# A hybrid three-mixer diffusion layer with MoE on one core: recurrence gates directly behind their projections, forget blocks next, output gate products within the HGRN2 levels, and the output projection in rows

## The reference

```python
sh1, sc1, gt1, sh2, sc2, gt2 = split(silu(c) @ ada_w + ada_b, 6)       # one set for context, one for latent
h = rms(x, norm1_w) * (1 + sc1) + sh1
qkv, g, a, b, q_hg, i_hg, g_hg, f_hg, x_rg, y_rg = split(h @ w_in)
o_a = gated_delta_net(qkv, g, a, b)      # 4 heads x 128, both directions
f = lb + (1 - lb) * sigmoid(f_hg)        # HGRN2: 4 heads x 64, both directions
o_b = rms(hgrn2(q_hg, i_hg, log(f))) * silu(g_hg)
u = dwconv(x_rg); r, i = sigmoid(u @ rg_gate_w + b)                    # RG-LRU, width 256
a_t = exp(-8 * r * softplus(-lam)); h_t = a_t * h_(t-1) + sqrt(1 - a_t**2) * (i * u)
o_c = (h_forward + h_backward) * gelu(y_rg)
x = x + gt1 * (concat(o_a, o_b, o_c) @ w_out)
h = rms(x, norm2_w) * (1 + sc2) + sh2
x = x + gt2 * moe(h)                     # 16 experts, top 2 within one group of 4
y = rms(x, final_norm_w)                 # and the final context states of the three mixers
```

## Time and profile before

| what | value |
|---|---|
| median of 3 runs | 1136.64 us (1133.79 to 1137.53) |
| the profiled execution's own time | 1141.2 us |
| its span | 1139.5 us |
| TensorE matmul busy | 944.6 us (83%) |
| VectorE busy | 429.4 us (38%) |
| ScalarE busy | 279.1 us (24%) |
| GpSimd busy | 125.5 us (11%) |
| share of the chain that ended last | TensorE 67%, VectorE 16%, ScalarE 5%, DMA 5%, issue 5% |

### The profile page before, as it was taken

The page is one execution under the profiler, slowest core; times in us unless marked ns, Lnnn a source line. Parts: engine busy times, 40 slices in busy tenths (PEclk is TensorE's granted clock), DMA queues, the critical chain, the costliest instruction groups (busy, mean ns, idle before and its releaser), DMA issues.

```text
span 1139.5 us, 24022 instructions
## 1 busy us (share of the span) xinstructions
PE 944.6 (83%) x10893; PEld 674.9 (59%) x10893; DVE 429.4 (38%) x718; ACT 279.1 (24%) x451; POOL 125.5 (11%) x138
## 2 busy tenths in 40 slices
PE   3799994458999889879999859966799999999930
PEld 3557753356665544678899845536667855765510
DVE  2340076996345233366577441137001000100008
ACT  3320534223112117222222230043201001100114
POOL 1300000000000000163555000000100000000021
PEclk9899997688999899989999969988899999999975
DMA  8990224266020200000000011255479999999835
GB/s 307 395 324 11 74 74 148 76 223 223 5 78 8 85 1 2 1 3 3 21 3 2 3 70 79 74 203 203 164 263 344 403 389 387 397 391 405 333 123 203
DMA packets 54413, 185.22 MB, mean 163 GB/s; under 512 B 8123, under 2 KB 11266, under 8 KB 50210
## 3 DMA queue, kind: packets, MB, share of 16 engines
q1 hardware_dynamic: 39408, 151.13, 34.9%
q0 software_dynamic: 6224, 22.55, 5.9%
q10 hardware_dynamic: 8674, 9.94, 2.5%
HBM read 160.93 MB, written 22.68 MB: 161 GB/s over the span
## 4 chain that ended last, share of the span: by engine, by line
PE 67%; DVE 16%; ACT 5%; DMA 5%; issue 5%; POOL 1%; ACTq 1%; DVEq 0%; POOLq 0%; SPq 0%
PE ps L657 19%; PE ps L1104 14%; PE ps L1127 7%; PE ps L925 7%; PE ps L723 6%; PE ps L647 4%; PE ps L913 3%; DMA arena<-in_moe_w_gate 1%; DMA ring<-in_ada_w 1%; PE ps L882 1%; ACT hT L1227 1%; PE ps L1001 1%; DVE arena L1885 1%; PE ps L796 1%; PE ps L1004 1%
## 5 line engine op out<-in xcount | busy, mean ns | idle before, releaser
L657 PE MATMUL ps<-hT,ring 128*128 128x128 f32 (+1 forms) x832 | 231.9, 439 | 3.2 <-ACT hT L1227 1.9
L657 PEld LDWEIGHTS ps<-hT,ring 128*128 128x128 f32 x832 | 126.4, 193 | 101.1 <-issue 96.8
L2310 DVE TENSOR_TENSOR hT<-ps,hT 128x384 f32<-128x384 f32 (+3 forms) x18 | 9.1, 506 | 248.1 <-ACT hT L1541 237.5
L1104 PE MATMUL ps<-ring,arena 128*32 128x128 f32 (+3 forms) x1104 | 87.6, 378 | 2.9 <-issue 1.8
L1104 PE MATMUL ps<-arena 128*32 128x256 f32 (+3 forms) x1360 | 85.5, 394 | 4.8 <-DVE arena L2302 2.5
L1104 PEld LDWEIGHTS ps<-arena 128*32 128x32 f32 (+1 forms) x1360 | 66.5, 114 | 24.4 <-issue 9.2
L1104 PEld LDWEIGHTS ps<-ring,arena 128*32 128x32 f32 (+1 forms) x1104 | 61.3, 118 | 29.0 <-issue 22.2
L723 PE MATMUL ps<-ring,hT 128*128 128x256 f32 (+1 forms) x240 | 69.2, 450 | 0.0
L647 PE MATMUL ps<-ident,arena 128*128 128x128 f32 (+3 forms) x278 | 41.7, 305 | 23.6 <-DVE arena L2086 10.8
L1694 POOL DMA_INDIRECT arena<-h_rows,slot_tok x18 | 16.6, 925 | 404.9 <-PE ps L647 234.6
L723 PEld LDWEIGHTS ps<-ring,hT 128*128 128x128 f32 x240 | 45.6, 190 | 23.7 <-issue 19.6
(11 more groups left out here) (416 smaller groups left out, 1340.0 us busy)
## 6 DMA issues: line engine op xcount, KB each, us to landing
ring<-in_ada_w SPq DMA_DIRECT2D x12, 2048.0 KB, 9.0
arena<-in_moe_w_gate SPq DMA_DIRECT2D x9, 2048.0 KB, 10.7
arena<-in_moe_w_up SPq DMA_DIRECT2D x9, 2048.0 KB, 15.4
arena<-in_moe_w_down SPq DMA_DIRECT2D x9, 2048.0 KB, 20.8
ring<-in_w_in SPq DMA_DIRECT2D x7, 2048.0 KB, 12.6
ring<-in_moe_w_gate SPq DMA_DIRECT2D x7, 2048.0 KB, 12.2
ring<-in_moe_w_up SPq DMA_DIRECT2D x7, 2048.0 KB, 15.4
ring<-in_moe_w_down SPq DMA_DIRECT2D x7, 2048.0 KB, 20.9
```

Of the source, the lines that this page charges most:

```text
L657: last = mm(out, w[:, k, cols], rhs(k)[:, a:b], start=(k == 0), stop=(k == KD - 1))
L1104: last = mm(ps[rows_of(n, g), GU, 512 * i + at:512 * i + at + width], m_xgT[:, b % 2, k, rows_of(n, j)], w[:, k, col:col + width], start=( ...
```

## The change

Four things are moved, and one stage is written anew.

1. `rgg` comes directly behind `rgy`; then `hq`, `hf`, one `ada`, `hi`. The slab plan has `hf` in one slab of 512 columns, and `hgate`'s weights get a load of their own into x's old place.
2. `hgate` is cut into five jobs of one tile each, behind the `ada` of levels 0 to 4. `ada` l+5 (before: l+6) follows level l. ScalarE copies `hgate` unchanged within its loop over the levels and applies Silu once, later. The forget gates' clamps, logs and additions go block by block.
3. The output projection is done in rows: ten jobs `("out", half, tile)` with tokens stationary and 512 output columns moving. The residual, the second norm and its scale and shift are done in rows, with the gate, scale and shift vectors loaded by DMA: a new job `modrow` turns them to rows, ScalarE stores them in DRAM, and SP loads them back spread over 128 partitions (`rows_in`), with x itself. `h2T` transposes each finished tile for the router product `logits`. `rms` 1, `router`, `h2row`, `rowvec` and `xrow` are gone.
4. The zero rows for the MoE's unused slots are stored from GpSimd's queue behind the load of `state_gdn` instead of at about 41 us, and the 16 small loads of the RG-LRU gate weights are issued by GpSimd, ahead of its `iota`s, instead of by ScalarE. SP issues the stores of h2, and expert 1 is loaded before the rest of expert 0.

```diff
@@ job_plan
     j += [("rgx", b) for b in range(2)] + [("rgy", b) for b in range(2)]
-    j += [("hq", b) for b in range(2)] + [("hi", n) for n in range(2)] + [("hgate", n) for n in range(2)]
     j += [("rgg", n) for n in range(8)]
-    j += [("hf", n) for n in range(4)]
-    j += [("ada", 4), ("ada", 5), ("adaT", 4)]
+    j += [("hq", b) for b in range(2)] + [("hf", n) for n in range(4)]
+    j += [("ada", 4)] + [("hi", n) for n in range(2)] + [("adaT", 4)]
     for l in range(8):
-        j += [("lev", l, n) for n in range(3)] + [("adaT", 4 + l)] * (l > 0) + [("ada", 6 + l)] * (l < 6)
-    j += [("qkv", 0)] + [("kdt", t) for t in range(NT)]
+        j += [("lev", l, n) for n in range(3)] + [("adaT", 4 + l)] * (l > 0) + [("ada", 5 + l)] * (l < 7) + [("hgate", l)] * (l < NT)
+    j += [("qkv", 0)] + [("kdt", t) for t in range(NT)] + [("modrow", 0)]
...
+def out_order():
+    a, b, c, d, e = ROW_ORDER
+    return [("out", 1, t) for t in ROW_ORDER] + [
+        ("out", 0, a), ("out", 0, b), ("h2T", a), ("out", 0, c), ("logits", a), ("h2T", b), ("out", 0, d), ("out", 0, e),
+        ("h2T", c), ("logits", b), ("h2T", d), ("logits", c), ("h2T", e), ("logits", d), ("logits", e)]
@@ SP
+            sp.wait_ge(*full_after(LAST[("out", 1)]))
+            first_expert(0, 1)
+            for n, t in enumerate(ROW_ORDER):
+                if t == ROW_ORDER[-1]:
+                    sp.wait_ge(*full_after(LAST[("out", 0)]))
+                    first_expert(0, 2)
+                sp.wait_ge(s_h2, n + 1)
+                sp.dma_start(h2_dram[P * t:P * t + P, :], m_h2[:, t, :]).then_inc(s_h2_stored, 16)
@@ ScalarE
+            for dp in range(4):
+                act.wait_ge(s_b_m, dp + 1)
+                ch(A(b_f[:, dp, :], b_f[:, dp, :], ACT.Ln))
+                A(b_Z[0][:, dp, :], b_Z[0][:, dp, :], ACT.Ln, scale=1.0 / LNSPLIT).then_inc(s_b_ln, 1)
             modulation(4)
-            modulation(5)
+            for n in range(2):
+                name = ("hi", n)
...
             for l in range(7):
                 act.wait_ge(s_b_d, l + 1)
                 A(b_f[:, :, :], b_f[:, :, :], ACT.Exp).then_inc(s_b_e, 1)
-                if l:
-                    modulation(5 + l)
+                modulation(5 + l)
+                if l < NT:
+                    name = ("hgate", l)
+                    act.wait_ge(*full_after(name))
+                    A(b_g[:, l, :], bank(name)[:, 0:256], ACT.Copy).then_inc(pair_free[pair(name)], 1)
...
+            def squared(t):
+                act.wait_ge(s_x1, ROW_ORDER.index(t) + 1)
+                r = small[:, 24 + t:25 + t]
+                ch(A(m_h2[:, t, :], x_rows[:, t, :], ACT.Square, accum_out=r))
+                ch.sync()
+                A(r, r, ACT.Sqrt, scale=1.0 / D, bias=small[:, 0:1]).then_inc(s_x1r, 1)
@@ VectorE
+            def x1_half(half, t):
...
+                TT(out=m_h2[:, t, at], in0=bank(name)[:, 0:512], in1=gate_row[min(t, 1)][:, at], op=MULT).then_inc(pair_free[pair(name)], 1)
+                dve.wait_ge(*free_after(name))
+                return TT(out=x_rows[:, t, at], in0=x_rows[:, t, at], in1=m_h2[:, t, at], op=ADD)
+            def h2_row(t):
...
+                link(V.reciprocal(r, r))
+                link(STT(out=m_h2[:, t, :], in0=x_rows[:, t, :], scalar=r, in1=scale_row[min(t, 1)], op0=MULT, op1=MULT))
+                TT(out=m_h2[:, t, :], in0=m_h2[:, t, :], in1=shift_row[min(t, 1)], op=ADD).then_inc(s_h2, 1)
+            dve.wait_ge(s_rows_in, 16 * 8)
...
+            dve.wait_ge(s_h2_stored, 16 * NT)
             link(V.tensor_reduce(m_col[:, 0:NT], m_p[:, :, :], AX.X, MAX))
```

More of the change, by code:

```diff
@@ L708, in _ @@
                 project(("rgy", b), w, slice(256 + P * b, 256 + P * b + P))
+            pe.wait_ge(s_conv_c, 2)
+            pe.wait_ge(s_wg_in, 16 * 16)
+            for n in range(8):
+                name = ("rgg", n)
+                pe.wait_ge(*free_before(name))
+                for a, b, out, g in segs(name):
+                    last = mm(out, c_wg[:, n, :], c_u[:, n % 2, a + 2 * g:b + 2 * g], start=True, stop=True)
+                last.then_inc(pair_full[pair(name)], 1)
             w = slab(("hq", 0))
@@ L713, in _ @@
                 project(("hq", b), w, slice(P * b, P * b + P))
+            w = slab(("hf", 0))
+            pe.wait_ge(*slab_after(("hf", 0)))
+            for n in range(4):
+                project(("hf", n), w, slice(P * n, P * n + P))
             def token_rows(kind, w, col, width, per, tiles=NT):
@@ L815, in _ @@
                 last.then_inc(pair_full[pair(name)], 1)
+            name = ("modrow", 0)
+            pe.wait_ge(s_scl2, 1)
+            pe.wait_ge(*free_before(name))
+            for g in range(2):
+                tr(bank(name)[0:48, P * g:P * g + P], modT[:, :, g])
+                last = tr(bank(name)[0:KD, 256 + P * g:384 + P * g], scl2[:, :, g])
+            last.then_inc(pair_full[pair(name)], 1)
             b_kdr = b_k.rearrange("p a t -> p (a t)").rearrange("p (t c n) -> p t c n", t=NT, c=4)
@@ L1036, in h2_rows, with h2_transposed @@
                 for k in range(KD):
-                    last = tr(bank(name)[:, P * k:P * k + P], hT[:, k, P * t:P * t + P])
+                    last = mm(bank(name)[:, 0:512], mix(k, t), slab(("out", half))[:, k, :], start=(k == 0), stop=(k == KD - 1))
                 last.then_inc(pair_full[pair(name)], 1)
-            for t in range(3):
-                h2_rows(t)
+            def h2_transposed(name):
+                pe.wait_ge(s_h2, ROW_ORDER.index(name[1]) + 1)
+                pe.wait_ge(*free_before(name))
+                for k in range(KD):
+                    last = tr(bank(name)[:, P * k:P * k + P], m_h2[:, name[1], P * k:P * k + P])
+                last.then_inc(pair_full[pair(name)], 1)
@@ new lines, in logits @@
+            def logits(name):
+                n = ROW_ORDER.index(name[1])
+                pe.wait_ge(s_narrow_in, 32)
+                pe.wait_ge(*free_after(("h2T", name[1])))
+                pe.wait_ge(*free_before(name))
+                for k in range(KD):
+                    last = mm(bank(name)[:, 0:NE], h2T[n % 2][:, k, :], cs[:, k, 0:NE], start=(k == 0), stop=(k == KD - 1))
+                last.then_inc(pair_full[pair(name)], 1)
+            for name in out_order():
+                {"out": out_rows, "h2T": h2_transposed, "logits": logits}[name[0]](name)
@@ L1318, in _ @@
             A(small[:, 8:12], small[:, 8:12], ACT.Ln, bias=small[:, 1:2]).then_inc(s_c_ln, 1)
-            for n in range(2):
-                name = ("hgate", n)
-                act.wait_ge(*full_after(name))
-                A(b_g[:, 4 * n:min(NT, 4 * n + 4), :], bank(name)[:, 0:256 * (4 if n == 0 else 1)]
-                       .rearrange("p (t c) -> p t c", c=256), ACT.Silu).then_inc(pair_free[pair(name)], 1)
-            act.wait_ge(s_z_stored, 16 * (1 + len(GAPS)))
             for n in range(8):
@@ L1343, in _ @@
                 allow_slow_non_contiguous=True).then_inc(s_state_stored, 16)
+            for b in range(2):
+                name = ("hq", b)
+                act.wait_ge(*full_after(name))
+                for a, e, out, g in segs(name):
+                    ins = A(b_q[:, b, a:e], out, ACT.Copy)
+                    ch(ins) if g == 0 else ins.then_inc(pair_free[pair(name)], 1)
             act.wait_ge(s_c_done, 1)
@@ new lines, in h2_copied @@
+            def h2_copied(t):
+                n = ROW_ORDER.index(t)
+                if n >= 2:
+                    act.wait_ge(*full_after(("logits", ROW_ORDER[n - 2])))
+                name = ("h2T", t)
+                act.wait_ge(*full_after(name))
+                A(h2T[n % 2], bank(name).rearrange("p (k t) -> p k t", k=KD), ACT.Copy).then_inc(pair_free[pair(name)], 1)
+            for n, t in enumerate(ROW_ORDER):
+                squared(t)
+                if n in (1, 2):
+                    h2_copied(ROW_ORDER[n - 1])
```

342 lines of the change are left out of this document (148 added, 194 removed).

## The result

The changed kernel takes 1143.76 us in the median of 6 executions (1140.93 to 1145.85), the kernel before 1136.39 in 6 executions beside it (1132.53 to 1139.00). The ratio is 1.0062, 95% interval 1.0032 to 1.0092: slower by 0.6%. The forecast was 1140.0, slower the likeliest sign; its mechanism was found in the trace as it was described.

What follows compares the result with a forecast made beforehand. TensorE bounds the kernel first, then a hole, VectorE in the levels, TensorE again from the output projection. +6.5 us behind the levels less 3.1 for projection and routing gives +3.4: median 1140.0 us, range 1134 to 1147 (61%).

Steps and rivals of the forecast that it cites:

- The recurrence and the levels: Up to the levels' first exponential: gain 39.2 us from the earlier recurrence; in the levels: loss 44.1 us, 102.1 against 58.0.
- the turn: One level as a single chain: E, PSUM copy, `ada`, `hgate`, its copy, exponential, Z; 17.3 us for each of four levels.
- No coupling in the levels: Rival, levels: exponential l+1 runs beside PSUM out, levels stay at 9.2 us, total 1098; chance 6%.
- The start: Kernel start: 16 loads ahead of the `iota`s and their 0.25 MB in 256-byte pieces cost +1.3 us (0 to 3).
- 0.3 us for `modrow` and the last exponential: Between the levels and the next stage: 0.3 us added, within that stage's later start of 6.5 us.
- the ring: Levels: ScalarE copies `ada` and `hgate` ahead of the next exponential, so parallel work becomes one chain, 17.3 us a level.
- 12.1 us: Last tile after the output projection, up to the maximum over the logits: 12.1 us, where it was 19.3.
- The output projection's: Output projection in rows: 68.7 us of matmuls, cold start 1.9, -0.5, two `h2T` of 0.95, one `logits` 2.2; ends 3.6 later.
- `hgate` at the lower clock: Rival, levels: `hgate` behind idle time runs slower, 3.1 us more in each of five levels, total 1155.5; chance 10%.
- The 16 loads ... at 0.51 us each: Start: GpSimd issues them before the `iota`s, 8 us in all, so the first modulation block starts 3 us late.
- The coupling was not short: Rival, levels and routing: `ada` at 2.0, `hgate` at 3.45, routing at its better bound, total 1128 to 1133; chance 20%.
- The rows were not late: Rival, output projection: row loads, seven reading one row 128 times, land after 711 us, total 1150 and more; chance 3%.

Runs made afterwards that it cites:

- the first experiment: Changed kernel, but ScalarE copies modulation block and output gate product behind the next level's exponential instead of ahead of it; 1102.93 us, ratio 0.9695 to the kernel before.
- the third experiment: Kernel before, but ScalarE copies each modulation block ahead of the next level's exponential instead of behind it, no work added; 1161.69 us, ratio 1.0215.
- the sixth experiment: The first experiment's kernel, with ScalarE's exponential after the levels ahead of block 11's copy and VectorE taking block 11 behind the last differences; 1099.02 us.
- the fourth and ninth experiments: Fourth: changed kernel, GpSimd's 16 gate-weight loads behind its index tables, 1143.64 us. Ninth: kernel of the eighth experiment, those loads behind the scaled input, 1097.16 us.
- the eighth experiment: Kernel of the sixth experiment, but ScalarE computes the first exponential of the levels ahead of its two value projection copies; 1097.90 us, ratio 0.9654.

## Why the prediction came out as it did

By its own steps, forecast against the profile of the kernel after:

| step | forecast | measured |
|---|---|---|
| start | +1.3 | +1.6 at the copy of `rgy` (81.24, before 79.65) |
| end of the first exponential, with the start | 167.1 | 167.95 |
| levels, 58.0 before | 102.1 | 102.35 |
| from there to the transposes of the keys | +0.3 | +2.3 (20.9 us against 18.6) |
| stage behind the levels starts later by | 6.5 | 9.4 to 9.6 |
| output projection, 71.15 before | +3.6 | +2.8 |
| last tile to the maximum over the logits, 19.3 before | 12.1 | 16.0 |
| routing chain | +0.5 | +0.7 |
| first gather | 0 | -2.0 |
| sum at the first gathered tokens | +3.4 | +7.6 |

**The recurrence and the levels were right.** The gain of the early recurrence (37.1 us at the first exponential, start included) and its loss in the levels (44.4) came as forecast. The gain is read from the two traces; no run moves the recurrence alone. The experiments show the cause of the loss: without the order of the copies the median falls by 40.8 us, with it alone the kernel before loses 24.0. Within the turn two terms missed in opposite directions: the `ada`s behind levels 1 to 5 took 3.26 to 3.64 us where I had 3.29, and the last copy cost 0.28 where I had 0.45. "No coupling in the levels" would have been 1098; it fell, and is nearly what the kernel became once ScalarE's order was mended.

**The start was right in part by luck.** TensorE's first projection begins 0.4 us later than before (43.32, before 42.90), and from there to the copy of `rgy` the same projections take 1.2 us longer. Windows of the kernel after, of the first experiment's and of the third's, from the first projection to that copy (length, busy PE, PEld, DVE, ACT, POOL; PEclk, DMA share, GB/s):

```profile
43.32:81.24 37.92, 37.92 (x131) 21.26 (x132) 12.44 (x34) 12.66 (x22) 0.00 (x0) 0.92 0.35 122
43.15:79.89 36.74, 36.74 (x131) 20.59 (x132) 12.44 (x34) 12.73 (x22) 0.00 (x0) 0.95 0.36 126
43.61:81.52 37.91, 37.91 (x131) 21.22 (x132) 12.35 (x34) 12.77 (x23) 6.26 (x13) 0.92 1.03 362
```

The length goes with the granted clock, 0.92 or 0.95, and not with the loads: the first experiment's kernel has the loads at the start and is short, the third's has the start of the kernel before and is long. So the 16 loads moved the fourth block by about 1 us, and most of the +1.6 at the end of the stage is a clock that my sum didn't have.

**"0.3 us for `modrow` and the last exponential"** was mis-sized by 2 us. I had followed the ring to the last Z and not beyond. The exponential behind the levels stands behind the copy of block 11 in the same way; the sixth experiment takes that wait out and gains 3.9 us.

**"12.1 us" for the last tile** was mis-sized by 3.9 us. The step took each `logits` at 2.2 us, from a row of ten matmuls, and a copy that follows at once. The timeline of the kernel after at this place, then windows of the second kind (length, busy PE, PEclk, DMA share, GB/s) on it:

```profile
765.78 1.86 PE L1094 MATMUL ps<-st,hT 128*128 128x16 f32 x16
...
769.05 3.32 PE L1094 MATMUL ps<-st,hT 128*128 128x16 f32 x16 [0.49 <-issue]
772.21 1.95 PE L690 MATMUL ps<-ident,arena 128*128 128x128 f32 x8
773.95 6.85 PE L1094 MATMUL ps<-st,hT 128*128 128x16 f32 x32
...
765.60:767.70 2.10, 2.10 (x22) 1.00 0.96 248
769.05:772.40 3.35, 3.35 (x17) 0.54 1.02 418
773.90:780.90 7.00, 6.89 (x34) 0.50 0.69 201
```

The first `logits` behind the projection runs at 2.4 GHz, the others after short idle times at 1.2 GHz, 3.4 us each. Three of them and one `h2T` make 5.5 us more than at the rates of the first `logits` and of the `h2T` at 767.5 us (1.07). That the clock makes the difference is read from these rows, not tried. The page of the Trainium skill that gave a rival, "TensorE: Matmul & The Clock Gate", Part 1 (The HAM clock gate), has the throttled clock as the default that only sustained activity lifts; here the trace agrees, with 0.54 and 0.50.

**The output projection's** terms don't add up to the +3.6 of the text: 68.7 + 1.9 - 0.5 + two `h2T` of 0.95 + 2.2 are 74.2 us, +3.1; measured +2.8. In the same way six projections of 8.7 are 52.2 us, not the 51.9 of the sum for the first exponential. Neither changes the sign.

**"`hgate` at the lower clock"**, the rival from that page, fell: 3.72 to 3.73 us behind the `ada`s of levels 1 to 4 (4.14 behind the first), where the row at full clock gave 3.45. The rival took the page's sentence to mean that the idle time ahead of the `ada` would hold `hgate` at the lower clock too; in the trace the `ada` between them was granted 0.50 to 0.57 and the `hgate` behind it 0.99 to 1.00 (levels 1, 2 and 4). The sentence by itself doesn't say which product the clock rises in; the profile's rows decided.

**"The 16 loads ... at 0.51 us each"** explained the late first block rightly. That it is the loads' own traffic and not GpSimd's queue which moves the slab of the fourth block (the prediction's third slab) was said beside it and is shown by the fourth and ninth experiments. Whether the 256-byte pieces cost more than their bytes is not shown: the loads delay that block by about 1 us, and 0.26 MB of the slabs themselves would take 0.7 at the 386 GB/s that the DMA view shows for most of that stretch. The Trainium skill's page "DMA: Bandwidth & Descriptors" (Specifications) wants at least 512 bytes a transfer for line rate. No run here tests that: the DMA view counts 512 packets for the 0.26 MB, 512 bytes each in the mean, and no kernel moved the same bytes in larger pieces.

**The gather** came 2.0 us sooner behind its indices than before; no step of mine had it. The windows show DMA engines at 0.27 in the routing after (0.58 before), but no run separates the causes, and it stays open. It is luck for the forecast: without it the places in time would differ by 9.6 us.

The other rivals fell too. The coupling was not short: the turn took 17.49 us. The rows were not late: TensorE is busy all of the 73.95 us of the projection, and VectorE's first sum of it, at 699.89, waits for TensorE alone.

## What to carry to other kernels

When two engines alternate in a loop, write down for each engine what stands ahead of the instruction that the other one waits for, and ask of each whether it needs something of this turn. A copy of the former turn's product was free here, a copy of this turn's closed a ring; the profile books the wait on the copy and leaves the exponential's own row without one. And when the bounding engine's busy time stays and its stage grows (57.3 us of 58, then 57.6 of 102), look for a wait and not for a lack of speed; here it was this ring.

## What the runs showed of the hardware

- ScalarE's table load doesn't wait for the semaphore of the exponential for which it is made: at 154.05 us in the eighth experiment, 9 us ahead of the exponential. Behind a copy that waits (164.3 in the changed kernel) the same 1.28 us stand in the chain.
- TensorE's clock adds to the cost of idle time. In the ring the `ada`s behind levels 1 to 5 took 3.26 to 3.64 us, each behind 7.44 us of idle time, at a mean granted clock of 0.78 in the stage. In the first experiment, with 50 us of work in 61, they took 1.95 to 2.39 at 0.94. How much of the shorter level is the clock's was not tried apart.
- The same work at the same place can differ by 1.2 us in 37 from one kernel's trace to another's, with the granted clock (0.92 or 0.95 from 43 to 81 us) and without an edit that explains it: the third experiment's kernel has the kernel before's code up to there.
